# Queries of the sample tokens to the latent space: four heads at a time in column groups, with swapped operands and turns

## The reference

```python
q_lat = jnp.einsum("bqhe,rhe->bqhr", q_nope, w_uk)        # 8 tokens, 8 heads: 128 -> 256
s_past = (jnp.einsum("bqhr,bkr->bhqk", q_lat, c_past)
          + jnp.einsum("bqhe,bke->bhqk", q_pe, kpe_past))
```

## Time and profile before

| | us |
|---|---|
| median of 3 runs | 1252.02 |
| lowest, highest | 1247.26, 1252.13 |
| the profiled execution, whole | 1253.11 |
| its span, first to last instruction | 1251.4 |
| its mean granted PE clock | 0.984 |
| busy: PE, DVE, ACT, POOL | 1177.7, 880.9, 634.8, 164.8 |

### The profile page before, as it was taken

How to read it: one execution, slowest core, us unless ns; L and a number is a source line. 1 busy time by engine, 2 the same in 40 slices (tenths; PEclk the granted TensorE clock), 3 DMA queues, 4 the chain that set the end, 5 groups by cost and what they waited for, 6 DMA issues and landing times. The chain is left out here.

```text
span 1251.4 us, 25114 instructions
## 1 busy us (share of the span) xinstructions
PE 1177.7 (94%) x9862; PEld 1079.6 (86%) x9862; DVE 880.9 (70%) x1519; ACT 634.8 (51%) x1087; POOL 164.8 (13%) x278
## 2 busy tenths in 40 slices
PE   5999999999989899998969999999998999999988
PEld 4998999999767799996859999999996679999867
DVE  5679888888756544666387988888896573449545
ACT  5583444444447444545654544444435564447444
POOL 2200101010353000031002010101014410002110
PEclk8998999999999999999989999999999999999999
DMA  7964656564567466695237666656554746668642
GB/s 216 249 173 132 177 135 177 135 178 129 165 173 209 131 181 188 193 303 206 84 103 202 199 166 181 167 145 167 146 151 144 213 144 186 181 183 244 230 153 70
DMA packets 319225, 216.08 MB, mean 173 GB/s; under 512 B 21621, under 2 KB 300513, under 8 KB 318811
## 3 DMA queue, kind: packets, MB, share of 16 engines
q1 hardware_dynamic: 302304, 166.74, 48.3%
q0 software_dynamic: 16480, 47.73, 12.1%
q10 hardware_dynamic: 330, 0.11, 0.0%
HBM read 209.31 MB, written 7.15 MB: 173 GB/s over the span
## 5 line engine op out<-in xcount | busy, mean ns | idle before, releaser
L1873 DVE TENSOR_TENSOR wlo<-stage,whi 128x2048 fp32r<-128x2048 f32 x140 | 320.5, 2289 | 170.5 <-ACT whi L1283 170.2
L1283 ACT ACTIVATE whi<-stage 128x2048 fp32r<-128x2048 f32 (+2 forms) x155 | 272.5, 1758 | 311.3 <-PE U L664 262.3
L662 PE MATMUL U<-Ahi,whi 128*128 128x264 f32 x1152 | 334.8, 291 | 7.9 <-issue 7.5
L663 PE MATMUL U<-Alo,whi 128*128 128x264 f32 x1152 | 329.0, 286 | 0.0
L664 PE MATMUL U<-Ahi,wlo 128*128 128x264 f32 x1152 | 328.5, 285 | 0.0
L662 PEld LDWEIGHTS U<-Ahi,whi 128*128 128x128 f32 x1152 | 219.6, 191 | 8.8 <-issue 7.7
L663 PEld LDWEIGHTS U<-Alo,whi 128*128 128x128 f32 x1152 | 219.7, 191 | 0.0
L664 PEld LDWEIGHTS U<-Ahi,wlo 128*128 128x128 f32 x1152 | 218.4, 190 | 0.0
L2040 DVE SCALAR_TENSOR_TENSOR acc<-uext,cwall,acc 128x256 f32<-128x256 f32 x464 | 188.6, 477 | 0.1
L662 PE MATMUL U<-Bhi,whi 128*128 128x264 f32 x384 | 109.1, 284 | 0.0
L663 PE MATMUL U<-Blo,whi 128*128 128x264 f32 x384 | 108.9, 284 | 0.0
(11 more groups left out here) (430 smaller groups left out, 2171.2 us busy)
## 6 DMA issues: line engine op xcount, KB each, us to landing
stage<-in_w_in SPq DMA_DIRECT2D x76, 1024.0 KB, 5.8
stage<-in_w_out SPq DMA_DIRECT2D x32, 1024.0 KB, 6.2
stage<-in_w_mk SPq DMA_DIRECT2D x8, 1024.0 KB, 6.8
cp<-in_cache_kv_latent POOLq DMA_DIRECT2D x64, 128.0 KB, 3.0
cp<-in_cache_kv_latent SPq DMA_DIRECT2D x64, 128.0 KB, 2.9
stage<-in_w_mv SPq DMA_DIRECT2D x8, 1024.0 KB, 5.6
Kt<-in_cache_mem_k POOLq DMA_DIRECT2D x16, 512.0 KB, 5.2
stage<-in_w_xq SPq DMA_DIRECT2D x8, 1024.0 KB, 7.3
```

Source lines behind the costliest of these rows:

```text
L662: mm(bk[:, 0:cols], whi[:, s, w], hi[:, k, :], start=(k == 0), stop=False)
L663: mm(bk[:, 0:cols], whi[:, s, w], lo[:, k, :], start=False, stop=False)
L1283: return A_(out, in_, ACT.Copy, scale=scale)
L1873: ins = V.tensor_tensor(wlo[:, s, :], stage[:, s, :], whi[:, s, :].bitcast(F32), ALU.subtract)
```

## The change

For each head the 8 sample columns of the queries are copied apart (`qn8`) and the turned `w_uk` goes to one of four buffers. Behind the scores of heads 3 and 7, four products follow, one per head: the stationary operand is now the 8 columns of `qn8`, the moving one the 256 columns of the turned `w_uk`, and the results go to partitions 32g to 32g+7 of HD, columns 256 to 511. DVE copies these 104 rows (`qlS`, in the place of the first of the four buffers), PE turns them in two pieces back into HD (`latent_turns`), and DVE copies the columns into `QLt` (`latent_columns`). The turns of the first group stand behind `head_turns(3)`, their copy behind head 3's lower output; those of the second group stand behind `new_columns(1)` and ahead of `unit(U_MK - 1)`, their copy behind `head_recip(7)`. Line 813 and the copy at line 2062 go away for each head. Two waits are replaced: PE's turns of `w_uk` wait for ACT's copy of the previous head, and for head 4 also for the column copy.

```diff
-    wukTS = at("wukTS", [P, 256], W + 36960)
+    wukT = [at(f"wukT{g}", [P, 256], o) for g, o in enumerate((W + 36960, W + 24256, B1 + 15 * T * 4, B0 + 15 * T * 4))]
+    qlS = at("qlS", [96 + NB, KVL], W + 36960)
+    qn8 = at("qn8", [P, 4, NB], W + 28544)
...
+    ql_mm, ql_ev = C("ql_mm", 4), C("ql_ev", 4)
...
-                pe.wait_ge(ql_ev.sem, ql_ev.at(l, h))
+                pe.wait_ge(wkT_ev.sem, wkT_ev.at(l, h))
+                if h == 4:
+                    pe.wait_ge(ql_ev.sem, ql_ev.at(l, 2))
...
-                pe.wait_ge(wkT_ev.sem, wkT_ev.at(l, h + 1))
+                if h % 4 == 3:
+                    pe.wait_ge(wkT_ev.sem, wkT_ev.at(l, h + 1))
+                    for g in range(4):
+                        last = mm(HD[32 * g:32 * g + NB, 256:512], qn8[:, g, :], wukT[g][:, :], start=True, stop=True)
+                    last.then_inc(ql_mm.sem, 1)
+
+            def latent_turns(q):
+
+                pe.wait_ge(ql_ev.sem, ql_ev.at(l, 2 * q + 1))
                 for c in range(2):
-                    last = mm(HD[:, 256 + NB * c:256 + NB * (c + 1)], wukTS[:, c * P:(c + 1) * P], qnS[:, TP:T],
-                              start=True, stop=True)
+                    last = tr(HD[:, 256 + c * P:256 + c * P + R], qlS[:, c * P:(c + 1) * P], ident[0:R, 0:R])
                 last.then_inc(ql_mm.sem, 1)
...
                 head_turns(h)
+                if h == 3:
+                    latent_turns(0)
                 unit(u + 3, 3, Ah, Al)
...
             new_columns(1)
+            latent_turns(1)
             unit(U_MK - 1, 1, Ah, Al)
             head_turns(H - 1)
-            wait_apart(pe, ql_ev.sem, ql_ev.at(l, H))
+            wait_apart(pe, ql_ev.sem, ql_ev.at(l, 4))
...
-                copy(wukTS[:, :], HD[:, 0:256]).then_inc(wkT_ev.sem, 1)
+                if h % 4 == 0:
+                    act.wait_ge(ql_mm.sem, ql_mm.at(l, h // 2))
+                elif h == 3:
+                    act.wait_ge(st_lat, l * 64 + 16)
+                copy(wukT[h % 4][:, :], HD[:, 0:256]).then_inc(wkT_ev.sem, 1)
...
+                copy(qn8[:, h % 4, :], HA[:, TP:T])
                 copy(qnS[:, :], HA[:, 0:T]).then_inc(qn_ev.sem, 1)
...
-            def head_latent(h):
-                dve.wait_ge(ql_mm.sem, ql_mm.at(l, h + 1))
-                V.tensor_copy(QLt[:, :, :, h], HD[:, 256:272].rearrange("p (c b) -> p c b", b=NB)).then_inc(ql_ev.sem, 1)
+            def head_latent(q):
+                dve.wait_ge(ql_mm.sem, ql_mm.at(l, 2 * q + 1))
+                V.tensor_copy(qlS[:, :], HD[0:R, 256:512]).then_inc(ql_ev.sem, 1)
+
+            def latent_columns(q):
+                dve.wait_ge(ql_mm.sem, ql_mm.at(l, 2 * q + 2))
+                V.tensor_copy(QLt[:, :, :, 4 * q:4 * q + 4].rearrange("p c b g -> p c g b"),
+                              HD[:, 256:512].rearrange("p (c g x) -> p c g x", c=2, x=32)[:, :, :, 0:NB]
+                              ).then_inc(ql_ev.sem, 1)
...
                 lo(u + 3, 1)
-                head_latent(h)
+                if h == 3:
+                    head_latent(0)
...
                     head_lower(h)
+                    if h == 3:
+                        latent_columns(0)
                     taps(h + 1, 15, 19)
...
             head_max(H - 1)
-            head_latent(H - 1)
+            head_latent(1)
             head_recip(H - 1)
+            latent_columns(1)
             lo(U_MK, 0)
```

More of the change, by code:

```diff
@@ L278, in build @@
     qn_mm, qn_ev, kv_mm, kv_ev = C("qn_mm", H), C("qn_ev", H), C("kv_mm", H), C("kv_ev", H)
-    sc_mm, ql_mm, ql_ev, ex_rdy, p_rdy = (C(n, H) for n in ("sc_mm", "ql_mm", "ql_ev", "ex_rdy", "p_rdy"))
+    sc_mm, ex_rdy, p_rdy = (C(n, H) for n in ("sc_mm", "ex_rdy", "p_rdy"))
+    ql_mm, ql_ev = C("ql_mm", 4), C("ql_ev", 4)
     m_rdy = C("m_rdy", 2 * H)
```

## The result

| | before | after |
|---|---|---|
| median, us | 1250.98 | 1257.82 |
| lowest, highest | 1247.26, 1254.63 | 1252.75, 1266.05 |
| the profiled execution, whole | 1253.11 | 1256.98 |
| its span | 1251.4 | 1255.3 |
| its mean granted PE clock | 0.984 | 0.982 |

Each median is over 20 runs on one chip. The ratio is 1.0054, with a 95% interval from 1.0039 to 1.0068: slower by 6.8 us. The interval leaves out 1, so the kernel is slower, though by half a percent only. Forecast were +5.6 us and 1257.6.

What follows compares the result with a forecast made beforehand. PE's own queue, busy 94% of the span, was taken as the bound. Before head 7 -4.0, head 7 +6.2, clock +3.4 sum to +5.6 us on the 1252.0 median: 1257.6, range 1250 to 1262.

Steps and rivals of the forecast that it cites:

- rival 4: Head 7: no wait, DVE copies in time or the shift is taken back; faster than before, 1248.9 us; chance 0.06.
- Heads 1, 2, 4, 5, 6: PE queue of these heads: two f32 products removed per head, 0.46 us saved each, 2.3 per layer.
- Heads 3 and 4: Head 3 pays 0.44 us for products and turns less its saving; head 4 waits 0.13 for DVE's column copy, per layer.
- Before head 7: Heads 0 to 6: 2.3 us off in layer 0, 2.0 in layer 1; with head 4's wait about -4.0 over both.
- Head 7's wait: Ahead of the second group's two turns PE stands still 4.1 us for DVE's copy of the latent rows, per layer.
- What comes back at the two old waits: Head 7, score turns and values: waits of 0.58 and 0.55 us vanish (1.13), plus 0.3 of matmul overlaps, per layer.
- Clock: Behind head 7's wait idle PE loses clock: 1.7 us per layer, 3.4 in all, with 0 and 6.8 as ends.
- rival 2: Unit after the new columns: low clock twice as long at both waits, 3.4 us more, 1261.0 us; chance 0.20.
- Rival 1: Head 7: the wait opens but the clock stays up, 3.4 us less than forecast, 1254.2 us; chance 0.17.
- Rival 3: Products of heads 0 to 3: column groups run one after the other, 2.2 us more, 1259.8 us; chance 0.07.
- its second form: At each of two tiling switches around the products, a pause of a matmul's length, 0.38 us: 1.2 more, 1258.8 us.
- Rival 5: Head 0: low clock ends sooner because sparse 8-column products are gone, -1.7 us within any case; no chance given.

Runs made afterwards that it cites:

- the first experiment: Changed kernel with head 7's two turns behind the unit, their copy behind DVE's gate product, first memory columns ahead of new-latent turns: 1248.71 us, 0.9977 against the kernel before.
- the direct measurement: Kernel with the turns behind the unit and head 4's column copy earlier, all four products of a group put in one column group: 1249.83 us, 0.9990 against before.

## Why the prediction held

**The mechanism** was the forecast's: the two turns ask for DVE's copy 4 us before DVE can give it, the unit stands behind them, and both waits behind the unit vanish. That the wait alone does this is shown by adding it to the kernel before (+9.1 us locally), and that the rest of the change does not, by the first experiment, which keeps every instruction and is faster than before (1248.7; rival 4, the kernel without the wait, was put at 1248.9).

**The time** of 1257.6 for a measured 1257.82 is closer than the forecast was, and that is luck: it started from the median of three runs, 1252.0, where twenty give 1250.98, and its difference, +5.6 for +6.8, was short by about as much.

**The terms**, each against its measure:

- *Heads 1, 2, 4, 5, 6: 0.46 each.* 0.42 to 0.45. Head 0 of the second layer: 0.08 for a forecast 0.1. Head 0 of the first layer: 0.43 for 0.44, but this agreement says nothing, as the distance differs by 1.2 us between two executions of the same code (33.63 and 32.44).
- *Heads 3 and 4: 0.44 + 0.13 = 0.57.* 0.57 in the first layer, 0.56 in the second, by two errors that cancel. Head 4's wait is 0.25 and not 0.13, since PE asks at 222.88, one matmul behind the last of the unit, and starts at 223.09 (0.21). DVE's copy ended at 222.94, as early as was forecast; PE started 0.15 us behind it, where 0.06 was taken; why it is more here is open. The rest is 0.32 and not 0.44: the eight products fit in 0.55 where 0.64 was taken, the unit's second matmul stands 0.23 behind its first where it was 0.20, and the two turns take 0.20 where 0.26 was. That 0.26 came from three turns behind a wait (0.39); three that follow other work without one take 0.25.
- *Before head 7: -2.3 and -2.0, with head 4's wait -4.0.* -2.05 and -1.71, -3.8 in all.
- *Head 7's wait: 4.1.* 3.95 and 4.16. *Start of the unit: +4.55.* From scores to unit it is 3.24 before (320.91 to 324.15) and 7.71 after: +4.47. *What comes back at the two old waits: 1.13 and 0.3.* From unit to turns +0.82 (7.45 for 6.63), of which the forecast has 1.7 - 0.73 = 0.97; from turns to values -0.77 (1.45 for 2.22), forecast -0.70. Values to page scores: -0.10, forecast 0.
- *Clock: 1.7 per layer, ends 0 and 3.4.* 1.6 in the first layer and 2.4 in the second. This term is short by 0.5 us in all, the most of any, and rival 2, the low clock twice as long at both waits, was right of one layer by its length. But a part of its 6.8 us at 1.2 GHz fell inside the wait itself, where a slow clock costs nothing. Finer windows of the kernel after put the fall at about 940.6, 1.6 us ahead of the turns:

```profile
940.50:941.00 0.50, 0.00 (x0) 0.00 (x0) 0.47 (x2) 0.00 (x0) 0.23 (x1) 0.57 0.00 0
941.00:942.14 1.14, 0.00 (x0) 0.00 (x1) 1.05 (x4) 0.34 (x2) 1.00 (x3) 0.50 0.38 111
942.14:947.00 4.86, 4.86 (x23) 4.86 (x24) 2.83 (x4) 2.30 (x8) 4.10 (x8) 0.50 0.81 228
```

Paid are 6.8 - 1.6 = 5.2 us, by half 2.6, beside the 2.4 measured. The forecast said that low time costs half of itself while PE is busy, and priced rival 2 as if it always were.

- *ACT's extra copies, the DMA queues: nothing.* No wait of PE for `qn8` or the queries appears after; head 1 to 2 has no room for it in its 0.44.

Local sum forecast 5.6, measured 6.1 (of which -0.43 is head 0's in the first layer), by the medians 6.8 (over its interval, 4.9 to 8.5).

**The rivals.** Rival 1, the clock stays up, is the kernel filled with nine products: +3.5 us by the ratio, beside the +2.2 it was given, and it did not happen on its own in any of the four waits of about 4 us. Rival 3, the column groups one after the other, is closed by the direct measurement; so is its second form: with both switches in it the whole group fits in 0.55. The Trainium skill, TensorEngine Tiling (Array Packing), section Key Properties, says that changing the tiling mode drains the engine. In these traces the first of the eight starts 0.63 us behind the product ahead of it, where it was 0.62 before the change, and the start of the next instruction is 0.55 us behind the first of the eight, for the 0.49 per eight inside the run of the earlier trace rows. So a drain, if there is one, costs less than 0.1 us here. Rival 4, faster than before, needed a wait under 3.0 us; the change had no such place, but it is 7 us away in the same queue. Rival 5 can't be read here: the low clock behind head 0's wait lasts 6.8 us after as before, but over the eight profiled executions it lasts, directly behind that wait, 6.8 or 6.9 us in four, 3.4 in one and none in three, and one of these three has the sparse products of before.

## What to carry to other kernels

Batching small products of several heads trades PE time for a round trip through another engine, and the round trip is priced by that engine's queue at the moment it is asked, not by the 0.4 us of its copy. Put the instruction that waits for it behind the next long block of work that doesn't need it: here moving two turns behind one unit, with the small copy behind them and the columns that cover it, turned a loss of 0.5% into a gain of 0.2%, and moving the other group's copy gave 0.25 us per layer more. In PE's queue everything behind the wait waited with it, and in five of the six waits of 2.2 to 4.2 us the idle time was charged again as low clock on what followed.

## What the runs showed that was not expected

- The clock's answer to nearly the same wait is not one number. In six waits of this study at the same place: 3.95 us idle, 3.4 us low; 4.16, 6.8 low; 3.79, 6.8; 3.80, 3.4; 2.20, none; 2.42, 3.4. The layer with the long low time changed sides between two kernels. For a wait of about 4 us a forecast would do better with two values, some 1.7 and 2.6 us, than with one; four such waits, two of each kind, are too few for their chances. The wait ahead of head 0's scores in the first layer tells the same: 1.64 us long both before and in the kernel with only the wait, it was followed by 6.8 us of low clock in one and none in the other.
- Low clock that ran while PE idled cost nothing: of 6.8 us in the second layer 5.2 were paid, by half. The kernel with only the wait agrees: with 2.9 us taken off in one layer and 1.7 in the other, 2.2 and 2.3 us are left for the wait, near the 3.80 - 1.43 that the forecast's own terms make of it.
- Three turns took 0.39 us of the queue behind a wait (330.78 to 331.17) and 0.25 without one (208.36 to 208.61). A length taken from a row behind a wait is too long for a place without one.
- Work made to cover an idle engine can pay for itself: 18 unused instructions in place of idle time took 3.9 us off head 7 in the two layers' traces (3.0 by the medians), without moving the instruction that ended the wait.
- Weights that arrive late for one unit of the memory stage cost up to 2.9 us, differently from one profiled execution to the next, and low clock far from the change comes and goes as well. A single pair of profiled executions is off by several us for that alone; of the 6.8 us by the medians it shows 3.9.
